# Projections and FFN of a two-block transformer kernel: three rounded products of split weights replaced by one plain 32-bit product

## What is computed

```python
# first block
h    = rms_norm(x, g);  proj = h @ w_in            # 1024 x 2304
y    = concat(window_attention(...), differential_attention(...))
x    = x + rms_norm(y @ w_out, g)                   # 1024 x 1024
u    = rms_norm(x, g) @ w_up                        # 1024 x 8192
c    = conv over 3 tokens (u) + b;  g, val = split(c)
x    = x + rms_norm((gelu(g) * val) @ w_down, g)    # 4096 x 1024
# second block
mod  = silu(c_2) @ w_ada + b_ada                    # 1024 x 6144, one row
qkv  = modulate(rms_norm(x), mod) @ w_in_2          # 1024 x 3072
x    = x + gate * (concat(dilated, stick_breaking) @ w_out_2)
x    = x + gate * mixture_of_32_experts(modulate(rms_norm(x), mod))   # each 3 x (1024 x 512)
out  = rms_norm(x)
```

## Time and profile before

| | us |
|---|---|
| median of three runs | 1022.28 |
| lowest, highest | 1022.24, 1025.56 |
| profiled execution, span | 1022.7 |
| PE busy in it | 995.2 |
| DVE, ACT, POOL busy | 551.4, 343.1, 79.7 |

### The profile page before, as it was taken

The page is one execution under the profiler, slowest core; times in us unless marked ns, Lnnn a source line. Parts: engine busy times, 40 slices in busy tenths (PEclk is TensorE's granted clock), DMA queues, the critical chain, the costliest instruction groups (busy, mean ns, idle before and its releaser), DMA issues.

```text
span 1022.7 us, 15498 instructions
## 1 busy us (share of the span) xinstructions
PE 995.2 (97%) x5996; PEld 699.2 (68%) x6006; DVE 551.4 (54%) x1043; ACT 343.1 (34%) x572; POOL 79.7 (8%) x118
## 2 busy tenths in 40 slices
PE   8999999999999999999999999999999999999997
PEld 6998799999999998989865544444444444443442
DVE  8557689889999997748435422222222222222222
ACT  5555664545355454337251211111110111110112
POOL 7200110111111200200002000000000000000000
PEclk9999999999999999899999999999999999999999
DMA  8334266797889744255656899999999999999993
GB/s 299 124 124 165 80 251 235 273 337 294 302 294 353 292 166 164 85 206 205 270 224 212 334 358 428 411 430 427 427 429 428 428 424 429 429 429 429 427 423 163
DMA packets 60007, 312.15 MB, mean 305 GB/s; under 512 B 4118, under 2 KB 5499, under 8 KB 47419
## 3 DMA queue, kind: packets, MB, share of 16 engines
q1 hardware_dynamic: 52160, 284.83, 69.6%
q0 software_dynamic: 7392, 26.54, 7.4%
q10 hardware_dynamic: 410, 0.16, 0.1%
HBM read 310.47 MB, written 1.05 MB: 305 GB/s over the span
## 4 chain that ended last, share of the span: by engine, by line
PE 86%; DMA 6%; DVE 4%; ACT 2%; issue 1%; POOL 1%; SPq 0%; DVEq 0%
PE bank L898 12%; PE bank L900 12%; PE bank L899 12%; PE bank L1405 10%; PE bank L1433 10%; PE bank L1389 9%; PE bank L1333 6%; DMA eslots<-in_w_up 4%; PE bank L1045 3%; PE bank L1350 3%; DMA ring<-in_w_in 2%; PE bank L973 1%; PE bank L1011 1%; PE bank L1205 1%; DVE ring_r L1850 1%
## 5 line engine op out<-in xcount | busy, mean ns | idle before, releaser
L898 PE MATMUL bank<-hT_r,ring_r 128*128 128x256 f32 x664 | 189.7, 286 | 1.1 <-DVE ring_r L1850 1.1
L900 PE MATMUL bank<-hT_r,ring_r 128*128 128x256 f32 x664 | 188.2, 283 | 0.0
L1850 DVE TENSOR_TENSOR ring_r<-ring,ring_r 128x2048 fp32r<-128x2048 f32 (+1 forms) x74 | 164.3, 2255 | 11.9 <-ACT ring_r L1511 11.5
L1511 ACT ACTIVATE ring_r<-ring 128x2048 fp32r<-128x2048 f32 (+1 forms) x74 | 136.6, 1889 | 38.8 <-DMA ring<-in_w_up 34.2
L899 PE MATMUL bank<-v_tok_r,ring_r 128*128 128x256 f32 x496 | 140.4, 283 | 0.0
L898 PEld LDWEIGHTS bank<-hT_r,ring_r 128*128 128x128 f32 x664 | 127.8, 192 | 1.9 <-DVE ring_r L1850 1.3
L900 PEld LDWEIGHTS bank<-hT_r,ring_r 128*128 128x128 f32 x664 | 127.7, 192 | 0.0
L1405 PE MATMUL bank<-eslots,scratch 128*64 128x512 f32 x512 | 114.5, 600 | 5.4 <-issue 3.0
L1433 PE MATMUL bank<-eslots,scratch 128*64 128x512 f32 x496 | 113.4, 595 | 0.7 <-ACT scratch L1740 0.7
L1389 PE MATMUL bank<-eslots,scratch 128*64 128x512 f32 x512 | 112.7, 592 | 0.0
L2331 DVE TENSOR_TENSOR scratch<-scratch,bank 128x512 f32<-128x512 f32 x16 | 11.0, 688 | 158.9 <-PE bank L1405 158.9
(11 more groups left out here) (306 smaller groups left out, 1466.9 us busy)
## 6 DMA issues: line engine op xcount, KB each, us to landing
eslots<-in_w_gate SPq DMA_DIRECT2D x31, 2048.0 KB, 25.4
eslots<-in_w_up SPq DMA_DIRECT2D x30, 2048.0 KB, 19.9
eslots<-in_w_down SPq DMA_DIRECT2D x28, 2048.0 KB, 24.0
ring<-in_w_up SPq DMA_DIRECT2D x16, 2048.0 KB, 11.7
ring<-in_w_in SPq DMA_DIRECT2D x9, 2048.0 KB, 7.8
ring<-in_w_down SPq DMA_DIRECT2D x8, 2048.0 KB, 9.4
kT<-in_w_ada POOLq DMA_DIRECT2D x24, 512.0 KB, 7.6
ring<-in_w_out SPq DMA_DIRECT2D x4, 2048.0 KB, 8.3
```

Of the source, the lines that this page charges most:

```text
L898: pe.matmul(dst, lhs[0], rhs[0], start=start, stop=False, **flags)
L900: return pe.matmul(dst, lhs[1], rhs[0], start=False, stop=stop, **flags)
L1511: sc.activation(hi, raw, ACT.Copy).then_inc(s_whi, 1)
L1850: last = ve.tensor_tensor(lo, raw, hi, ALU.subtract)
```

## The change

`split`, `product`, `rounded` and `low` go. PE multiplies the loaded weights with unrounded activations, one plain 32-bit product in place of three rounded ones. The activations of a turn are written by ACT and DVE in alternate pairs of tiles (`activations`). The ring holds six chunks: chunk n waits for chunk n-6. The FFN, which was a loop for PE, ACT, DVE and SP, is written out. The product of gate and value goes to one of two buffers in `hn` (`act`). The order in which experts use the ten places changes with the ring (`ESLOTS`).

The core of the diff:

```diff
-            def split_ready(n, more=0):
-                pe.wait_ge(s_wlo, n + 1 + more)
-            def product(dst, lhs, rhs, start, stop, **flags):
-                pe.matmul(dst, lhs[0], rhs[0], start=start, stop=False, **flags)
-                pe.matmul(dst, lhs[0], rhs[1], start=False, stop=False, **flags)
-                return pe.matmul(dst, lhs[1], rhs[0], start=False, stop=stop, **flags)
+            def weights_ready(n):
+                pe.wait_ge(loaded[slot_for(n)], loads_until(n))
+            def activations_ready(tag, k):
+                pe.wait_ge((s_hT, s_hA)[by_scalar(tag, k)][tag], done_count(tag, k))
...
                             for k in range(KD):
-                                last = product(PS[2 * part + b][:, f * S:(f + 1) * S], both(w, k, c, P),
-                                               tiles("ffn", k), start=(k == 0), stop=(k == KD - 1))
+                                if i == part == b == f == 0:
+                                    activations_ready("ffn", k)
+                                last = pe.matmul(PS[2 * part + b][:, f * S:(f + 1) * S], w[:, k, c:c + P], hT[:, k, :],
+                                                 start=(k == 0), stop=(k == KD - 1))
...
             def straight(n, src):
-                load(n % LANES, src, consumed(n - LANES) if n >= LANES else None)
+                load(slot_for(n), src, consumed(n - SLOT_N) if n >= SLOT_N else None)
...
-            with sp.Fori(2, CHUNKS - 1) as i:
-                for c, (src, free) in enumerate(zip(ffn_chunks(i), ((s_up, 4 * (i - 1) + 2), (s_up, 4 * (i - 1) + 4),
-                                                                    (s_down, i - 1)))):
-                    load((seq_gate(1) + c) % LANES, src, free)
+            for i in range(1, CHUNKS):
+                for c, src in enumerate(ffn_chunks(i)):
+                    straight(seq_gate(i) + c, src)
...
+            def activations(tag, scale, shift=None):
+                for k in range(*TURN_K[tag]):
+                    if by_scalar(tag, k):
+                        continue
+                    ve.wait_ge(s_turn[tag], turn_count(tag, k))
+                    src = turned_tile(tag, k)
...
-                ve.tensor_tensor(conv[:, 0, :, :], conv[:, 0, :, :], conv[:, 1, :, :], ALU.mult).then_inc(s_prod, 1)
-                if not last:
-                    split(*((seq_gate(2) + 1, 3 * more) if later else (seq_gate(1) + 1,)))
+                if i >= 2:
+                    ve.wait_ge(s_down, i - 1)
+                ve.tensor_tensor(act[:, i % 2, :, :], conv[:, 0, :, :], conv[:, 1, :, :], ALU.mult).then_inc(s_act, 1)
                 modulate(7)
-                ve.wait_ge(s_ahi, i + 1)
-                ve.tensor_tensor(act_r[:, 1, :, :], conv[:, 0, :, :], act_r[:, 0, :, :], ALU.subtract)\
-                    .then_inc(s_act, 1)
```

More of the change, by code:

```diff
@@ L924, in project @@
                     pe.wait_ge((s_evA, s_evV)[m % 2][blk], m // 2 + 1)
[L925 to L934, removed]
+                if kind in ("q", "k", "ka"):
+                    c0 = where[1] if kind == "q" else where[0]
+                    for k in range(KD):
+                        last = pe.matmul(bank[:, 0:S], w[:, k, c0:c0 + P], hT[:, k, :], start=(k == 0),
+                                         stop=(k == KD - 1))
+                elif kind == "vt":
+                    for k in range(KD):
+                        last = pe.matmul(bank[:, :], hT[:, k, where[0] * P:(where[0] + 1) * P], w[:, k, :],
+                                         start=(k == 0), stop=(k == KD - 1))
+                else:
                     c0, cw, _ = where
@@ L944, in project_high_first @@
                 tag = ("attn1", "attn2")[blk]
[L945 to L948, removed]
+                assert all(it[0] == 0 and it[1] == "q" for it in ITEMS[blk][:count]) and count <= AHEAD[blk]
+                w = chunk_view(slot_for(n_base))
+                if blk == 0:
+                    pe.wait_ge(s_loaded_once, 16)
+                else:
+                    weights_ready(n_base)
@@ L955, in project_high_first @@
[L955 to L959, removed]
+                        c0 = ITEMS[blk][n][2][1]
+                        last = pe.matmul(item_bank(blk, n)[:, 0:S], w[:, k, c0:c0 + P], hT[:, k, :], start=(k == 0),
                                          stop=(k == KD - 1))
-                    last.then_inc(s_gemm[blk], 1)
+                        if k == KD - 1:
+                            last.then_inc(s_gemm[blk], 1)
@@ L1629, in taps @@
                     last = sc.activation(conv[:, part, 2 * b + f, :], PS[2 * part + b][:, f * S:(f + 1) * S],
[L1630 removed]
+                                         ACT.Identity, scale=vec[:, 1, ft:ft + 1], bias=vec[:, 1, ft + FT:ft + FT + 1])
                 last.then_inc(s_tap, 1)
[L1633 to L1635 removed]
+            sc.preload_act_table(ACT.Gelu_apprx_tanh)
+            for i in range(CHUNKS):
                 taps(i, 0, 0)
[L1637 removed]
                 taps(i, 0, 1)
@@ L1668, in _ @@
             sc.wait_ge(s_modc, 1)
-            rounded("attn2", lambda k: gmixc[:, k:k + 1], lambda k: modc[:, 0, k:k + 1])
-            split(N_IN2 + 2)
-            take(1, range(8))
-            split(N_IN2 + 3)
-            take(1, range(8, AHEAD[1]))
+            activations("attn2", lambda k: gmixc[:, k:k + 1], lambda k: modc[:, 0, k:k + 1])
+            take(1, range(AHEAD[1]))
             sc.preload_act_table_set("natural_log_exp_and_others")
@@ L2112, in modulation, with ffn @@
                                             dst, ALU.mult, ALU.add).then_inc(s_sum, 1)
-            def ffn(i, more=None, units=False, last=False, between=False):
-                later = more is not None
+            def ffn(i, units=False, between=False):
                 def modulate(*cs):
@@ L2162, in _ @@
             ffn(0, between=True)
-            with ve.Fori(1, CHUNKS - 1) as i:
-                ffn(i, i - 1, units=True)
-            ffn(CHUNKS - 1, CHUNKS - 2, last=True, between=True)
+            for i in range(1, CHUNKS - 1):
+                ffn(i, units=True)
+            ffn(CHUNKS - 1, between=True)
             ve.wait_ge(s_mod, 1)
```

403 lines of the change are left out of this document (104 added, 299 removed).

## The result

The changed kernel takes 1101.3 us (median of 4 runs, 1100.04 to 1102.67), the kernel before in the same series 1023.14 (1022.24 to 1025.56). The ratio is 1.0762, 95% interval 1.0742 to 1.0782: slower by 78 us, where I forecast 144 us faster. The profiled execution has a span of 1098.4 us. This was the third rival, to which I gave one chance in a hundred.

What follows compares the result with a forecast made beforehand. PE was taken to bound the kernel, with transfers taking over in the FFN. From 1022.7 us, -7 - 18 - 3.5 - 92 - 13 - 10 = -143.5 gave about 879 us, range 862 to 903.

Steps and rivals of the forecast that it cites:

- the third rival: Everywhere on PE: a plain product takes four passes, 0.43 us at 256 columns, 0.86 at 512; 1111 us, chance 0.01.
- the price of a plain product: On PE: 0.217 us at 256 columns, 0.43 at 512, against 0.36 and 0.68 for three rounded ones; 162 us less work.
- The spacing of the FFN's products: Sign in the FFN: plain products start 0.217 us (256 columns) and 0.43 us (512) apart; otherwise the prediction is wrong.
- The counts of products: Changed products on PE: 776 of 256 columns, 192 of 512 and 16 of 128.
- The FFN bound by transfers: FFN: transfers at 390 GB/s outlast PE's work, PE waits 13 us, the stage takes 180 us, -92 us.
- The first rival: FFN: PE alone decides, the stage takes 167 us and the kernel 866; chance 0.2.
- the second (350 GB/s): FFN: transfers bind harder, at 350 GB/s the stage takes 195 us and the kernel about 900; chance 0.27.
- The Trainium skill's 358 GB/s: Reference limit on transfers from HBM to SBUF; by it the FFN would end at about 192 us.
- The start: Start to first scores: cheaper items and no splits bring first scores to about 28 us, -7 us.
- The attention: Attention and output projection ahead of the FFN: cheaper products and fewer splits, -18 us and -3.5 us.
- The stick-breaking pass: Stick-breaking heads: a pass with a single item takes 3.9 us, the stage -10 us.
- The experts: From 512 us on: same products and same lead of loads, 450.4 us kept, change 0 (to +8).

Runs made afterwards that it cites:

- e1_prices: Only 48 products of each kind on PE, the kernel's computation left out: plain 0.432 us at 256 columns, 0.85 at 512; rounded 0.121 and 0.227.
- e2_two_passes: The changed kernel with each changed plain product made as two bf16 products of the words' upper halves, lower halves left out: 888.88 us, ratio 0.8685.

## Why the prediction was wrong

**The step that failed is the price of a plain product.** I wrote "Four of 256 columns take 1.03 us", "Thirteen of 128 columns", "Thirty-two of 512 columns take 13.93 us": I took the records of the earlier trace rows for products. The program has two products of 256 columns in a pass of such a unit, and 4 x 4 = 16 in the second half of the last output projection, where the trace has x4 and x32. So the row said 13.93/16 = 0.87 us for 512 columns all along, and 0.43 for 256. Both numbers were at hand, the count in the order of instructions and the count in the row; I never set one beside the other. The error is a factor of two in the sign-giving term: -162 us of PE's work became +88. The spacing of the FFN's products, the first sign of being wrong that I had named, is 0.432 and 0.858 us and not 0.217 and 0.43.

**The reference that I overruled was right.** The Trainium skill (FP8 and Floating Point Precision, TensorE Precision Notes) gives true 32-bit four passes. e1_prices has 0.85 us against 0.216 for one bf16 pass of 512 columns, 3.9. I wrote that the trace showed two; it showed two records for a product, each with the time of two bf16 products (0.432/2 = 0.216, against 2 x 0.109).

**The third rival** named the price (0.43 and 0.86) and its effect: "89 us, 1111 us". Measured were +78. What it left out is the 7 to 13 us that the rest of the change gave back.

**The counts of products** (776, 192, 16) were right: with the measured price they give the table's last column. The stages of the prediction left out eight products of 256 columns and the 16 of 128 ahead of the first scores, 4.7 us of its own 162 us of PE.

**The FFN bound by transfers** did not come about, only because PE was slower than they. With nearly the assumed price (e2_two_passes) it did, at up to 402 GB/s and in 185 us. The first rival (FFN in 167) would have been wrong there, and the second (350 GB/s) too. The Trainium skill's 358 GB/s (DMA: Bandwidth & Descriptors, Where 436 GB/s comes from) is exceeded by the FFN's full slices in that run, 391 to 402 GB/s, as by the 427 to 429 of the experts in the earlier trace rows.

**The start** was mis-sized in the forecast, -7. In e2_two_passes first scores come at 31.72 (28 forecast), and the chain's row of the lambda vectors shows what was late: they land at 28.0, where the forecast had the 24.89 of the earlier trace rows, and PE waits 6.8 us for what follows from them (`kT`, by ACT).

**The attention** of e2_two_passes is 31.72 to 109.79, 78.1 us, against the 97.05 of before: -19 where -21.5 stood. **The stick-breaking pass** with one item took 3.96 us there (3.9 forecast). **The experts** kept their length: 448.9 us after the change.

## What to carry to other kernels

Before a price is read off a trace, set the count of records in the row beside the count of instructions in the program; if the trace has two for one, the price is that of both. A change whose whole gain is one unit price deserves that one comparison, or one run that measures it, before any stage by stage working; and when a reference and a row differ by a round factor, suspect the divisor first. Where an engine is at 98% of the span, what other engines and queues are relieved of gives back little: here splits, a second engine's work and three more places came to some 7 us of 1023, 13 by the most generous count. And a time per chunk is taken between like points of the chunks: first to first, not first to last.

## What the runs showed of the hardware

- A plain 32-bit product leaves two matmul records; from start to start it takes 0.432 us at 256 columns and 0.85 at 512, 3.6 and 3.7 times a rounded one (0.121, 0.227). At 128 columns it takes 0.224, 1.9 times a rounded one (0.119).
- A plain product of 64 columns took as long as one of 128, 0.22 us. In e1_prices the groups of 48 have the same busy time:

```profile
L65 PE MATMUL bank<-x_tok 128*128 128x128 f32 x96 | 10.9, 276 | 0.0
L63 PE MATMUL bank<-x_tok 128*128 128x64 f32 x96 | 10.8, 274 | 0.0
```

- A rounded product of 128 columns costs 5.87/48 = 0.12 us, as much as one of 256.
- bf16 products of 256 columns on strided halves of 32-bit words ran 0.114 us apart in the kernel, 0.109 on packed tiles alone. Whether the stride or the other work beside them is the reason was not tried.
- DVE's subtraction with a strided bf16 result in place took 2.65 us for 2048 columns, against 2.255 with the rounded 32-bit result of the earlier trace rows.
